# State-space output's first tables, attention's keys and first queries in space of their own, loaded during the projection ahead; the gate operand split block by block

## What is computed

```python
proj = rms_norm(x) @ w_in                      # q, k, v, g_ret, u, g_s5
ret = retention(q, k, v) * silu(g_ret)
y = gelu(S5(u) + d * u)                        # linear recurrence over the sequence
ssm = y * sigmoid(y @ glu_w + glu_b) * silu(g_s5)
x = x + concat(ret, ssm) @ w_out
qa = rms_norm(x) @ xa_wq;  ka = m @ xa_wk;  va = m @ xa_wv
p = softmax(qa @ ka.T * XA_DH ** -0.5)         # 4 heads, 1024 x 256
x = x + (p @ va) @ xa_wo
```

## Time and profile before

| | |
|---|---|
| time, median of 3 runs | 2987.63 us (2986.06 to 2989.02) |
| the profiled execution's own time | 2999.26 us |
| its span | 2997.4 us |
| busy: TensorE, VectorE, ScalarE, GpSimd | 89%, 39%, 18%, 23% of the span |
| granted TensorE clock, mean | 0.912 |

### The profile page before, as it was taken

One profiled execution on the slowest core, in us unless ns is written; L12 is line 12 of the kernel. 1 busy time (PEld: TensorE's weight loads), 2 busy tenths in 40 slices (PEclk: granted clock), 3 DMA queues, 4 the chain that ended last, 5 costly groups with the idle time before them and its releaser, 6 DMA issues.

```text
span 2997.4 us, 36256 instructions
## 1 busy us (share of the span) xinstructions
PE 2667.2 (89%) x15154; PEld 2190.3 (73%) x15154; DVE 1171.2 (39%) x1954; ACT 551.4 (18%) x877; POOL 700.0 (23%) x323
## 2 busy tenths in 40 slices
PE   6799999968977789996998979877798999999998
PEld 5588888856755568885787768665686888888887
DVE  7781177802646523402251223354423222222223
ACT  4111111103100001212141322344211000000002
POOL 2684132310110003321031211000303332222330
PEclk9899999969965579998999989798798999999999
DMA  7445432334221133143132334111301211111111
GB/s 239 133 148 169 143 107 94 106 102 134 93 76 58 55 120 99 45 153 119 57 120 91 100 106 131 50 45 55 142 0 43 67 45 56 42 42 42 48 43 56
DMA packets 204579, 267.84 MB, mean 89 GB/s; under 512 B 30017, under 2 KB 126242, under 8 KB 204450
## 3 DMA queue, kind: packets, MB, share of 16 engines
q1 hardware_dynamic: 172194, 217.63, 22.6%
q10 hardware_dynamic: 32256, 48.35, 4.3%
HBM read 192.44 MB, written 73.50 MB: 89 GB/s over the span
## 4 chain that ended last, share of the span: by engine, by line
PE 79%; DVE 11%; ACT 3%; POOL 2%; DMA 2%; issue 2%; SPq 1%; ACTq 0%; DVEq 0%; POOLq 0%
PE PS L444 23%; PE PS L2736 16%; PE PS L447 15%; PE PS L2753 8%; PE PS L1216 2%; PE PS L1471 2%; PE PS L1470 1%; POOL W_LO L414 1%; PE PS L1214 1%; PE PS L1477 1%; PE PS L1653 1%; PE PS L613 1%; PE PS L1673 1%; DVE T L899 1%; DVE T L900 1%
## 5 line engine op out<-in xcount | busy, mean ns | idle before, releaser
L408 POOL TENSOR_SCALAR W_HI<-RAW 128x2048 fp32r<-128x2048 f32 (+1 forms) x66 | 131.0, 1985 | 1622.5 <-PE PS L444 758.4
L444 PE MATMUL PS<-W_HI,OP_HI 128*128 128x512 f32 (+1 forms) x1184 | 306.0, 402 | 22.5 <-issue 9.2
L444 PE MATMUL PS<-W_LO,OP_HI 128*128 128x512 f32 (+1 forms) x1184 | 289.7, 387 | 0.0
L444 PE MATMUL PS<-W_HI,OP_LO 128*128 128x512 f32 (+1 forms) x1184 | 286.4, 384 | 0.0
L414 POOL TENSOR_TENSOR W_LO<-RAW,W_HI 128x2048 fp32r<-128x2048 f32 (+1 forms) x59 | 272.9, 4626 | 44.6 <-DVE W_LO L394 39.9
L444 PEld LDWEIGHTS PS<-W_HI,OP_HI 128*128 128x128 f32 x1184 | 223.4, 196 | 69.6 <-issue 12.3
L444 PEld LDWEIGHTS PS<-W_LO,OP_HI 128*128 128x128 f32 x1184 | 222.7, 191 | 45.4
L444 PEld LDWEIGHTS PS<-W_HI,OP_LO 128*128 128x128 f32 x1184 | 219.0, 188 | 43.7
L447 PE MATMUL PS<-OP_HI,W_HI 128*128 128x512 f32 (+1 forms) x768 | 191.0, 392 | 19.2 <-DVE OP_LO L1245 12.4
L466 ACT ACTIVATE OST<-PS 128x512 f32<-128x512 f32 (+2 forms) x164 | 94.6, 577 | 557.1 <-PE PS L447 288.8
L2736 PE MATMUL PS<-OP_HI,W_HI 128*128 128x512 f32 x704 | 176.0, 392 | 14.0 <-POOL W_LO L2718 14.0
(11 more groups left out here) (423 smaller groups left out, 3707.5 us busy)
## 6 DMA issues: line engine op xcount, KB each, us to landing
RAW<-in_w_in SPq DMA_DIRECT2D x28, 1024.0 KB, 5.2
RAW<-in_w_gate_up SPq DMA_DIRECT2D x44, 512.0 KB, 4.7
RAW<-in_w_out SPq DMA_DIRECT2D x12, 1024.0 KB, 5.3
RAWD<-in_w_down SPq DMA_DIRECT2D x11, 1024.0 KB, 4.9
x_d<-X SPq DMA_DIRECT2D x2, 4096.0 KB, 15.5
X<-x_d SPq DMA_DIRECT2D x2, 4096.0 KB, 12.8
ptok_d<-OST ACTq DMA_DIRECT2D x24, 256.0 KB, 2.0
pch_d<-OST ACTq DMA_DIRECT2D x24, 256.0 KB, 2.0
```

What stands on the lines that cost most here:

```text
L408: nc.gpsimd.tensor_scalar(hi, raw, 1.0, 1.0, ALU.mult, ALU.mult).then_inc(*w_hi.by(1))
L444: ins = nc.tensor.matmul(PS[:, bank, 0:width], act_part[:, k, (g.tile0 + a) * P:(g.tile0 + a + 1) * P], w_part[:, slot, k, 0:width], start ...
```

## The change

It does four things.

1. UY, TY and CY get two separate places outside OP_HI: block 0, 2, 4 and 6 in "extra", which is free after the S5 tables, and the odd blocks in "stage", where OST lies. UTy moves to "stage" too. SyncE loads block 0 right after the state-space input stage; for blocks 1 to 7 it waits for the stores of `gs5`.
2. The last two halves of `sp_weights(weights_before("glu"))` come behind all table loads. The same is done at attention with `weights_before("xo")`.
3. `act_split_y` and `dve_split_y` are gone. `y_gelu` makes OP_HI of its block right after gelu, and VectorE makes OP_LO of block q-1 (`dve_y_low`) behind the YS copies of block q.
4. KA moves to "x", where nothing is stored any more; VA and KA are issued together, the query tiles 0 to 3 wait for all but the last four stores of `xq` (the gemm does the first 512 tokens of a weight block first), and tile 4 for all.

```diff
-    UY = at("UY", "ophi", 0, [P, 2, SC, P])
-    TY = at("TY", "ophi", 8192, [P, 2, SC, P])
-    CY = at("CY", "ophi", 16384, [P, 2, 4, 2, P])
-    UTy = at("UTy", "ophi", 24576, [P, 8, P])
+    UY2 = (at("UYa", "extra", 0, [P, SC, P]), at("UYb", "stage", 0, [P, SC, P]))
+    TY2 = (at("TYa", "extra", 4096, [P, SC, P]), at("TYb", "stage", 4096, [P, SC, P]))
+    CY2 = (at("CYa", "extra", 8192, [P, 4, 2, P]), at("CYb", "stage", 8192, [P, 4, 2, P]))
+    UTy = at("UTy", "stage", 12288, [P, 8, P])
...
-    def sp_s5_y(sp):
-        sp.wait_ge(*s5_zero_out(16 * (SC - 1)))
-        sp.wait_ge(*mm_done(gemms["gs5"].end))
-        for q in range(8):
+    def sp_s5_y(sp, parts):
+        for q in parts:
             b = q % 2
+            if q == 0:
+                sp.wait_ge(*s5_zero_out(16 * (SC - 1)))
+                sp.wait_ge(*s5_r(NSL))
             if q >= 2:
                 sp.wait_ge(*s5y_mm(q - 1))
...
         act.activation(YO[:, q].rearrange("c n i -> c i n"), PS_T(6), ACT.Gelu_apprx_tanh).then_inc(*s5y_yo.by(1))
...
+        act.wait_ge(*s5y_yo(q + 1))
+        act.activation(OP_HI[:, q, :], YO[:, q].rearrange("c n i -> c (n i)"), ACT.Copy).then_inc(*la_hi.by(1))
+
+    def dve_y_low(dve, q):
+        dve.wait_ge(*la_hi(q + 1))
+        nc.vector.tensor_tensor(OP_LO[:, q, :], YO[:, q].rearrange("c n i -> c (n i)"),
+                                OP_HI[:, q, :].bitcast(F32), ALU.subtract).then_inc(*la_lo.by(1))
...
+            if q:
+                dve_y_low(dve, q - 1)
+        dve_y_low(dve, 7)
...
-    KA = at("KA", "stage", 0, [P, KT, MEM])
+    KA = at("KA", "x", 20736, [P, KT, MEM])
...
         sp.dma_start(VA[:, :, :], va_d.rearrange("(k p) n -> p k n", p=P)).then_inc(*xa_kv.by(16))
-        wait_stores(sp, "xq")
+        sp.dma_start(KA[:, :, :], ka_d.rearrange("(k p) m -> p k m", p=P)).then_inc(*xa_kv.by(16))
+        wait_stores(sp, "xq", more=-4)
         for t in range(TT):
             if t >= 2:
                 sp.wait_ge(*xa_s(t - 1))
+            if t == 4:
+                wait_stores(sp, "xq")
...
+            sp_s5_y(sp, range(1))
+            sp_weights(sp, weights_before("glu") - 2)
+            wait_stores(sp, "gs5")
+            sp_s5_y(sp, range(1, 8))
             sp_weights(sp, weights_before("glu"))
-            sp_s5_y(sp)
-            wait_stores(sp, "gs5")
...
-            sp_weights(sp, weights_before("xo"))
+            sp_weights(sp, weights_before("xo") - 2)
             sp.wait_ge(*x_out(16))
             sp_attention(sp)
+            sp_weights(sp, weights_before("xo"))
```

More of the change, by code:

```diff
@@ L1156, in build @@
     SCAN_END = 3 * NCH + 1
-    UY = at("UY", "ophi", 0, [P, 2, SC, P])
-    TY = at("TY", "ophi", 8192, [P, 2, SC, P])
-    CY = at("CY", "ophi", 16384, [P, 2, 4, 2, P])
-    UTy = at("UTy", "ophi", 24576, [P, 8, P])
+    UY2 = (at("UYa", "extra", 0, [P, SC, P]), at("UYb", "stage", 0, [P, SC, P]))
+    TY2 = (at("TYa", "extra", 4096, [P, SC, P]), at("TYb", "stage", 4096, [P, SC, P]))
+    CY2 = (at("CYa", "extra", 8192, [P, 4, 2, P]), at("CYb", "stage", 8192, [P, 4, 2, P]))
+    UTy = at("UTy", "stage", 12288, [P, 8, P])
+    URy = at("URy", "stage", 16384, [P, 8, P])
     YS = at("YS", "ophi", 28672, [P, SC, 8, SP_])
     YO = at("YO", "oplo", 0, [P, KT, NCH, SC])
-    URy = at("URy", "stage", 16384, [P, 8, P])
     s5y_ur = sem("s5y_ur")
@@ L1179, in sp_s5_y @@
             s = s5y_in1 if b else s5y_in0
-            sp.dma_start(UY[:, b], u_d.rearrange("(n j) c -> n j c", j=SC)[:, :, q * P:(q + 1) * P]).then_inc(*s.by(16))
-            sp.dma_start(TY[:, b], toep_d[:, :, q * P:(q + 1) * P]).then_inc(*s.by(16))
-            sp.dma_start(CY[:, b], cc_d[:, 4 * q:4 * q + 4, :, :]).then_inc(*s.by(16))
+            sp.dma_start(UY2[b][:, :, :], u_d.rearrange("(n j) c -> n j c", j=SC)[:, :, q * P:(q + 1) * P])\
+              .then_inc(*s.by(16))
+            sp.dma_start(TY2[b][:, :, :], toep_d[:, :, q * P:(q + 1) * P]).then_inc(*s.by(16))
+            sp.dma_start(CY2[b][:, :, :, :], cc_d[:, 4 * q:4 * q + 4, :, :]).then_inc(*s.by(16))
     def pe_s5_y(pe):
@@ L1213, in pe_s5_y @@
                 o = PS[:, 4 + g % 2, (g // 2) * P:(g // 2 + 1) * P]
-                T.matmul(o, UTy[:, g, :], TY[:, b, :, 16 * g:16 * g + 16], start=True, stop=False)
+                T.matmul(o, UTy[:, g, :], TY2[b][:, :, 16 * g:16 * g + 16], start=True, stop=False)
                 for c in range(2):
-                    ins = T.matmul(o, SCAN[lo:lo + 64, c, 4 * q + g // 2, 0:NCH], CY[lo:lo + 64, b, g // 2, c, :],
+                    ins = T.matmul(o, SCAN[lo:lo + 64, c, 4 * q + g // 2, 0:NCH], CY2[b][lo:lo + 64, g // 2, c, :],
                                    start=False, stop=c == 1)
@@ L1253, in regroup @@
             nc.vector.tensor_copy(URy[:, :, :].rearrange("n g (j c) -> n g j c", j=SC),
-                                  UY[:, q % 2].rearrange("n j (g c) -> n g j c", g=8)).then_inc(*s5y_ur.by(1))
+                                  UY2[q % 2][:, :, :].rearrange("n j (g c) -> n g j c", g=8)).then_inc(*s5y_ur.by(1))
         regroup(0)
@@ L1634, in sp_attention @@
                 sp.wait_ge(*xa_s(t - 1))
+            if t == 4:
+                wait_stores(sp, "xq")
             sp.dma_start(QTL[:, t % 2], qa_d.rearrange("(k p) t -> p k t", p=P)[:, :, t * P:(t + 1) * P])\
               .then_inc(*xa_q[t % 2].by(16))
-            if t == 0:
-                sp.dma_start(KA[:, :, :], ka_d.rearrange("(k p) m -> p k m", p=P)).then_inc(*xa_kv.by(16))
     def pe_attention_scores(pe):
@@ L2922, in _ @@
             act_s5_y(act)
-            act_split_y(act)
             retention = act_retention(act)
@@ L2951, in _ @@
             dve_s5_y(dve)
-            dve_split_y(dve)
             retention = dve_retention(dve, chain)
```

## The result

Median 2933.02 us (four runs, 2929.08 to 2940.59) against 2986.85 (2985.87 to 2989.02) for the kernel before: ratio 0.9822, 95% interval 0.9801 to 0.9843. Forecast was 2929.4, range 2910 to 2941. The profiled execution took 2940.59, 58.7 less than the profiled 2999.26 of before, where 58.2 was forecast. Two later groups of runs of the same kernel gave medians of 2936.15 and 2934.84. The distance between the medians is thus 50 to 54 us, and 2929.4 was 4 to 7 us too low.

What follows compares the result with a forecast made beforehand. TensorE bounds the kernel nearly everywhere, except two holes, at the starts of state-space output and attention. State-space output 39.8 + 8.0 - 2.3 - 7.6 = 37.9, plus attention 20.3, is 58.2 off 2987.63: 2929.4 us, range 2910 to 2941.

Steps and rivals of the forecast that it cites:

- First tables early: State-space output's start: block 0's tables loaded ahead, so TensorE starts at the last eviction instead of waiting; 39.8 us less.
- operand by block: State-space output's end: OP_HI and OP_LO made inside the loop, one pair left before the gate; 8.0 us less.
- Extra work hidden on ScalarE and VectorE: State-space output loop: the added 1.06 and 1.11 us per block of 10.73 hide; uncovered, up to 2.2 us per block.
- Block 1's set just in time, copy held, transposes at 626.65: State-space output: data arrive at 623.1, GpSimd holds the regroup copy until 626.5, delaying block 1; 2.3 us lost.
- One slow block, 7.6: State-space output: TensorE's 2.5 us idle before block 1 lowers the clock for one block; 7.6 us, from 0 to 15.
- The rival that let the clock fall at once: State-space output: low clock starts at block 0's short gaps and lasts three blocks or more; 2937 to 2952 us, chance 0.13.
- Attention, 20.3: Attention's start: early keys and queries save 28.1 us; VectorE held by GpSimd costs 5.1, a clock fall 2.7; net 20.3.
- The Trainium skill's rule against the 128x1 row: Attention tile 0: the rule has GpSimd hold L1707; by the 128x1 row it is not held and time is 7.3 lower.
- The slow rival (3025): State-space output and attention: the clock, once down, doesn't come back; 38 us slower, 3025; chance 0.02.
- late loads: Starts of state-space output and attention: the change fails to bring loads forward; some 2950 us, chance 0.03.
- from the profile to the median: Whole kernel: 58.2 us off the profiled 2999.26 gives 2941.1; the median counterpart, 11.6 lower, gives 2929.4.

Runs made afterwards that it cites:

- The kernel without GpSimd and gaps in the way: Changed kernel plus 14 constant transposes in TensorE's gaps around block 0, and GpSimd's split of the gate's second weight block after the state-space output: 2923.73 us, ratio 0.9796.
- the split by block alone: Read from the changed kernel with OP_HI and OP_LO made in one go behind the loop again: 2943.26 us, ratio 0.9846, beside the changed kernel's 2936.15.
- second profile: Profile of the unaltered changed kernel, run again beside its parts: that execution took 2935.02 us; the group's median was 2936.15, ratio 0.9829.
- attention-only kernel: Kernel before with only the attention part of the change (KA in x, early loads, two weight halves behind the query tiles): 2967.43 us, ratio 0.9931.
- extra transposes in attention too: All three edits with the output projection's splits waiting for attention's last tile, plus constant transposes around block 0 and in four attention gaps: 2936.44 us, ratio 0.9820.
- last-tile kernel: Changed kernel with transposes around block 0, later gate split, and GpSimd's splits of the output projection's second block held until attention's last tile: 2931.04 us, ratio 0.9811.
- operand-split kernel: Changed kernel with the gate operand's high and low parts made in one go behind the last block, as before: 2943.26 us, ratio 0.9846.
- later-split kernel: Changed kernel with GpSimd's splits of the output projection's second block held until attention's tile 0 has its scaled probabilities: 2934.83 us, ratio 0.9820.

## Why the prediction was right, and where it was off

- **First tables early, 39.8, and operand by block, 8.0:** right. The kernel without GpSimd and gaps in the way reached 94.5 us for the stage where the two terms give 93.2; the split by block alone measured 8.0 in the profiles and 7.1 in the medians.
- **Extra work hidden on ScalarE and VectorE:** right; with blocks at full clock the YS copies are 10.73 us apart in the profile after, the same as before.
- **Block 1's set just in time, copy held, transposes at 626.65:** right where block 0 runs at full clock: 13.75 us behind the projection's end in the second profile (613.67 to 627.42), 13.78 forecast. In the first profile the hold is there, at 3.77 us, and hidden.
- **One slow block, 7.6:** right in size and place in the second profile (18.34 us from block 1's transposes to block 2's, against 10.73). In the first its place was wrong: block 0, behind the two short gaps, not block 1 behind the gap of 2.5 us, and it cost less. The rival that let the clock fall at once was right about the start and wrong about the length: the clock was back after one block, where before it needed 40 us. An unbroken TensorE isn't the reason, as it had no hole from 639.9 to 677 in the profile of before either; the reason stays open, and that one block was taken from a span of 0 to 2 with nothing nearer is luck in part. Against 93.2, the profile's 99.95 is block 0's products (13.4 for 8.3, 5.1), the transposes of block 1 (1.90 for 1.09) and the last turn (1.88 for 1.11): 6.7. With the hold hidden the stage gave 41.05 us where 37.9 was forecast.
- **Attention, 20.3:** right. Transposes of tile 0 came 13.6 us behind the eviction's end (1311.22), 13.5 forecast; L1707 and L1711 were held by 0.8 and 4.0 us. The clock's fall cost 1.6 rather than 2.7 (64.8 us from those transposes to the output projection against 63.2 before). The transposes stand 14.2 us behind the query projection's end, 37.2 before; 23.0 less 1.6 is 21.4 in the profile, and the part alone 18.6 in the medians.
- **The Trainium skill's rule against the 128x1 row:** the rule decided rightly. L1707 on 128x4 was held wherever GpSimd stood beside it (0.94 to 2.51 us), as was the 128x8 of the earlier trace rows. That L1711, with two sources in SBUF, is held too the prediction had taken without a row of a two-source operation. The Trainium skill, "GPSIMD Engine Reference", key points, names VectorE instructions with two SBUF inputs among those that contend, and the trace agrees (5.28 us against 1.24).
- **The slow rival (3025) and late loads:** neither occurred; the clock came back in both stages.
- **The step that failed: from the profile to the median.** I took 58.2 off 2999.26 and off 2987.63 alike, as if the 11.6 us between the profiled execution and the median had nothing to do with these stages. A slow block of 7.6 us was in those stages: the untouched stage took 141.0 in the profile of before and 133.4 in the attention-only kernel's. So the state-space part is 41 us in the profiles and 30.1 in the medians, and the sum 48.7 to 54 rather than 58.2. That the old stage has two courses is inferred from two profiles; how often each occurs was not measured. How much of the 11.6 it makes up isn't known either, since the untouched stretch of the second block was long in the profile of before too (337.6 against 330.7 at the shortest).
- **The 58.7 between the profiles, where 58.2 was forecast,** is close by luck. The kernel after was 63.5 us ahead at the start of attention's output projection and 58.6 at the end: 4.1 were given back between that start and the first row of the untouched stretch, and 1.1 in the stretch.

## What to carry to other kernels

When a stage's start waits for loads, it's worth freeing two places for them; but then ask of every operation that moves earlier what GpSimd does at that moment, since a copy or a scale between SBUF tiles is held to the end of GpSimd's operation, and moving GpSimd's work instead can just move the hold to later operations, or delay a load that stands behind it on a queue, as both happened in attention. Where a profile shows stretches at the low clock, price the edit from an execution with and one without them, and don't carry the profile's excess over the median along as a constant: here a stage with a hole differed by 7.6 us between two profiles, and a stretch that no edit touched by 8.

## What the runs showed of the hardware

- **Two short gaps went with the low clock.** Behind gaps of only 0.7 and 1.1 us around 1.1 us of transposes the granted clock was at 0.50 from about 618 on in six of seven profiles (in one from about 617.5); in the seventh it stayed at 1.00 there and fell at a gap of 2.3 us. With fourteen transposes of a constant in the gaps block 0 ran at 1.00 in five of five. In one of these (extra transposes in attention too) the clock still dipped for a few us behind a gap of 0.69 us at block 1 (0.60 from 625.5 to 629.7), while in the last-tile kernel it stayed at 1.00 behind one of 0.75 us at the same place.
- **The way back took very different times** in the same stream of small fp32 products: 13 us in the profile after (618 to 631), about 22 in the second profile of the same kernel, 22 in the attention-only kernel's, 34 in the operand-split kernel's, and 40 in the profile of before. TensorE was busy without a hole throughout in the 13, in the 34, and in the last 37 of the 40. No run shows what decides it.
- **A held operation ends with GpSimd's, or up to about its own time behind it:** L1711 (1.24 alone) ended 1.1 us, the regroup copy (0.69 alone) 0.5 us behind GpSimd's operation; the scale on 128x4 (0.17 alone) right at its end. GpSimd's operations of 4.5 us took 4.49 to 4.53 in these places. But its short one (1.9 us) took 2.88 where it started, at 1327.21 in the later-split kernel, while a held multiply of VectorE was still running (to 1328.32).
- **A 128x1 operation was not held.** Of the 50 L540 on 128x1 in the profile of before, eight stand by themselves inside a GpSimd operation, and each took 0.14 or 0.15 us, as elsewhere.
